# A new opening of a two-block transformer kernel: order of the first transfers, the first panel by high products first, bucket rows as a plain transfer, bias rows moved

## The chip, the core and the metric

The kernel runs on one core of one Trainium2 chip. The metric is the device time of one execution in microseconds (us), as the median of the runs made. TensorE does the matrix products, VectorE and ScalarE the elementwise work, GpSimd a few small steps, and SyncE issues most transfers. In rows of the profile they are PE, DVE, ACT, POOL and SP; PEld is TensorE's weight load.

## What is computed

Two blocks on 256 tokens of width 1024, all in float32. The first has two attention branches (a windowed one, and one with three dilated groups), each with biases by relative position from a table of 32 buckets; the second block has two layers with another table. The opening of the program is the first norm and the first projections:

```python
h = rms_norm(x, norm_gain[layer])
proj = h @ w_in[layer]
qa, ka, va, qb, kb, vb, ga, gb, mg = jnp.split(proj, split_idx, axis=-1)
...
qa = head_rms_norm(qa.reshape(bsz, S, A_Q_HEADS, HEAD_DIM), q_norm_a[layer]) * scale
ka = head_rms_norm(ka.reshape(bsz, S, A_KV_HEADS, HEAD_DIM), k_norm_a[layer])
va = va.reshape(bsz, S, A_KV_HEADS, HEAD_DIM)
ya, _ = banded_attention(qa, ka, va, A_WINDOW, 1, rel_bias[:, :A_Q_HEADS], sink_a[layer])
...
bias = bias_table[t5_bucket(rel * stride)]
```

## The kernel before

**Products in parts.** Each float32 operand is split into a high part (rounded to the matmul's own type, float32r) and a low part (the rest), and each product is made of three matmuls: high by high, high by low, low by high. Weights arrive in halves of 128 x 2048 elements (1 MB) in a ring of six slots. For each half ScalarE rounds the high part (`round_half`, L569) into one of three high slots, and VectorE subtracts to get the low part (`low_half`, L611). The first half of the first panel is done in two pieces (L566, L567, L604, L607).

**Panels.** A panel is 256 tokens by 512 output columns, in one of two PSUM buffers that take turns: `qa` in panel buffer 0, `kava` (256 columns) in buffer 1, `qb0` in buffer 0 again, `qb1` in buffer 1. `rows_out` writes a panel: for each of eight chunks k of the inner dimension and two groups b of tokens it issues the three matmuls (L921, L922, L923), 48 in all. Before its first matmul it waits until the buffer is evicted. After some chunks it runs other work (`after`), by the chunk's number.

**The head norm.** `qa`, `kava`, `qb0` to `kb2` are normed by head. Once the panel is done, ScalarE writes its squares (L1512, scaled by `rstd`, the row norm of x), VectorE sums them (L1884), GpSimd takes the inverse root (L2407 and L2409, `inverse_root`, with a drain between the two), and VectorE writes the normed heads to `tok` (L1894). Only then is the panel buffer free. Later TensorE transposes the heads (`turn_heads`) and ScalarE evicts them (`evict_heads`, L1451).

**The first work.** ScalarE's queue brings `ident` (the identity for transposes) and `first` (gains); SyncE's queue brings x in two pieces, three halves of weights, four small bias tables, and more halves. TensorE waits for `ident` and `first`, then transposes x in four groups of four (L971); ScalarE evicts each with the gain as the high part (L1393) and VectorE makes the low part (L1803). The row norm of x goes ScalarE (L1365), GpSimd (L2407, L2409, L2417).

**Bias rows.** `onehot`, 65 x 4608 elements, says for each relative position which bucket it has. GpSimd's queue brings it (L2412) once the second half of weights has landed, and the transfer rounds it to float32r. Nine matmuls of the table with it (L1029, `head_bias_row`) give nine tiles of bias rows, which ScalarE evicts (L1421, `evict_bias_row`) and, after the third panel, stores to memory (`store_bias_rows`). `BIAS_AT` says after which panel and chunk each is done: the first after the last chunk of `qa`, the other eight after the eight chunks of `kava`. These tiles, those of x and those of the turned heads share three PSUM tiles in the order of `FIRST_TILES`.

## Time and profile before

| | |
|---|---|
| three runs | 1227.75, 1228.25, 1226.32 us; median 1227.75 |
| the profiled execution | 1226.56 us, of which 1224.8 us are the span between its first and last instruction |
| mean granted clock of TensorE | 0.989 |

The span is the time from the first to the last instruction. The profile of one execution gives for each engine its instructions with their start and duration. "Idle before" with an arrow names what ended the idle time of the engine.

### The profile page before, as it was taken

What the parts mean: (1) busy time and instruction counts of PE and PEld (TensorE: products, weight loads), DVE (VectorE), ACT (ScalarE), POOL (GpSimd) and SP (SyncE); (2) the same over time, 40 slices, a digit from 0 to 9 for tenths busy, and PEclk for the clock granted to TensorE, in tenths of its full rate; (3) what the DMA queues carried; (4) which work ended last, traced back from release to release, by engine and by line L of the source; (5) the groups of instructions that cost most, each with busy time, mean ns of one, the idle gap of its engine ahead of it and who ended that gap; (6) DMA issues with size and microseconds to landing.
All of it is one profiled execution on the core that took longest, in us unless ns stands there. A gap on an engine that the chain in (4) does not pass through costs nothing.

```text
span 1224.8 us, 17214 instructions
## 1 busy us (share of the span) xinstructions
PE 1174.8 (96%) x6879; PEld 1013.7 (83%) x6879; DVE 825.6 (67%) x1317; ACT 571.1 (47%) x701; POOL 46.0 (4%) x56
## 2 busy tenths in 40 slices
PE   6999998999999998899999999999998899999996
PEld 5888887887998776687999888998776778999885
DVE  4665465556689768887677554698678787776542
ACT  5645564454425745453534433535745443444331
POOL 0232000000000000000000000000000000000000
PEclk9999999999999999899999999999999999999998
DMA  9656653436545667454555655556557554554640
GB/s 313 210 183 234 219 156 120 134 132 257 173 146 206 176 179 193 141 175 169 176 193 183 205 196 196 167 172 221 158 158 189 154 175 169 179 198 174 217 144 35
DMA packets 41344, 219.73 MB, mean 179 GB/s; under 512 B 4311, under 2 KB 14039, under 8 KB 16615
## 3 DMA queue, kind: packets, MB, share of 16 engines
q1 hardware_dynamic: 39104, 204.62, 48.8%
q0 software_dynamic: 1824, 13.78, 5.9%
q8 instruction: 55, 0.90, 0.3%
q10 hardware_dynamic: 336, 0.22, 0.1%
q14 instruction: 25, 0.20, 0.0%
...
## 4 chain that ended last, share of the span: by engine, by line
PE 77%; DVE 11%; issue 3%; ACT 3%; DVEq 2%; DMA 2%; POOL 0%; POOLq 0%; ACTq 0%
PE panel L921 16%; PE panel L923 15%; PE panel L922 15%; PE panel L944 7%; PE panel L943 7%; PE panel L942 7%; DVE area L2075 3%; PE tile L971 3%; DVE ring_parts L611 3%; ACT ring_parts L569 1%; DMA ring_parts<-in_w_layers_dram 1%; PE heads_out L1132 1%; DVEq L2076 1%; PE panel L961 1%; PE panel L960 1%
## 5 line engine op out<-in xcount | busy, mean ns | idle before, releaser
L611 DVE TENSOR_TENSOR ring_parts<-ring,ring_parts 128x2048 fp32r<-128x2048 f32 (+1 forms) x173 | 388.0, 2254 | 172.5 <-ACT ring_parts L569 162.1
L569 ACT ACTIVATE ring_parts<-ring 128x2048 fp32r<-128x2048 f32 (+1 forms) x185 | 348.1, 1888 | 241.3 <-PE panel L923 184.2
L921 PE MATMUL panel<-ring_parts,hT_high 128*128 128x512 f32 (+2 forms) x688 | 282.5, 411 | 11.7 <-DMA ring_parts<-in_w_layers_dram 8.5
L923 PE MATMUL panel<-ring_parts,hT_low 128*128 128x512 f32 (+2 forms) x688 | 267.4, 389 | 0.0
L922 PE MATMUL panel<-ring_parts,hT_high 128*128 128x512 f32 (+2 forms) x688 | 266.7, 388 | 0.0
L942 PE MATMUL panel<-hT_high,ring_parts 128*128 128x256 f32 x704 | 199.4, 283 | 0.0
L944 PE MATMUL panel<-hT_high,ring_parts 128*128 128x256 f32 x704 | 199.3, 283 | 0.0
L943 PE MATMUL panel<-hT_low,ring_parts 128*128 128x256 f32 x704 | 199.3, 283 | 0.0
L921 PEld LDWEIGHTS panel<-ring_parts,hT_high 128*128 128x128 f32 x688 | 131.3, 191 | 44.8 <-issue 11.8
L923 PEld LDWEIGHTS panel<-ring_parts,hT_low 128*128 128x128 f32 x688 | 130.9, 190 | 27.5
L921 PE MATMUL panel<-ring_parts,area_parts 128*128 128x512 f32 x384 | 150.6, 392 | 0.0
L922 PE MATMUL panel<-ring_parts,area_parts 128*128 128x512 f32 x384 | 149.9, 390 | 0.0
L922 PEld LDWEIGHTS panel<-ring_parts,hT_high 128*128 128x128 f32 x688 | 131.6, 191 | 20.3
L923 PE MATMUL panel<-ring_parts,area_parts 128*128 128x512 f32 x368 | 143.7, 391 | 0.0
L942 PEld LDWEIGHTS panel<-hT_high,ring_parts 128*128 128x128 f32 x704 | 135.2, 192 | 0.0
L943 PEld LDWEIGHTS panel<-hT_low,ring_parts 128*128 128x128 f32 x704 | 135.2, 192 | 0.0
L944 PEld LDWEIGHTS panel<-hT_high,ring_parts 128*128 128x128 f32 x704 | 135.2, 192 | 0.0
L2075 DVE SCALAR_TENSOR_TENSOR area<-area,cw 128x256 f32<-128x256 f32 x240 | 100.2, 479 | 2.9
L921 PEld LDWEIGHTS panel<-ring_parts,area_parts 128*128 128x128 f32 x384 | 72.2, 188 | 15.2
L922 PEld LDWEIGHTS panel<-ring_parts,area_parts 128*128 128x128 f32 x384 | 72.2, 188 | 15.0
L923 PEld LDWEIGHTS panel<-ring_parts,area_parts 128*128 128x128 f32 x368 | 69.1, 188 | 14.8
L1706 ACT ACTIVATE area_parts<-area 128x1024 fp32r<-128x1024 f32 x16 | 17.0, 1060 | 98.7 <-DVE area L2374 98.7
...
## 6 DMA issues: line engine op xcount, KB each, us to landing
ring<-in_w_layers_dram SPq DMA_DIRECT2D x140, 1024.0 KB, 4.9
ring<-in_w_first_dram SPq DMA_DIRECT2D x40, 1024.0 KB, 5.2
ring_parts<-in_w_layers_dram POOLq DMA_DIRECT2D x12, 1024.0 KB, 8.7
...
area<-in_gains_dram SPq DMA_DIRECT2D x3, 512.0 KB, 5.8
```

The lines of the kernel that those rows point to most:

```text
L569: act.activation(ring_lo[:, SLOTS + hi, 0:w], ring[:, slot, 0:w], ACT.Copy).then_inc(high_ready, 1)
L611: g.tensor_tensor(ring_lo[:, slot, 0:w], ring[:, slot, 0:w], ring_lo[:, SLOTS + hi, 0:w], ALU.subtract).then_inc(low_ready, 1)
L921: pe.matmul(ps[:, b, 0:width], high, hi[:, k, :], start=first, stop=False)
L922: pe.matmul(ps[:, b, 0:width], high, lo[:, k, :], start=False, stop=False)
L923: mm = pe.matmul(ps[:, b, 0:width], low, hi[:, k, :], start=False, stop=last)
L942: pe.matmul(to, hi[:, k, cols], hT_hi[:, k, :], start=(k == 0), stop=False)
L943: pe.matmul(to, hi[:, k, cols], hT_lo[:, k, :], start=False, stop=False)
L944: mm = pe.matmul(to, lo[:, k, cols], hT_hi[:, k, :], start=False, stop=(k == KC - 1))
L960: pe.matmul(to, hi[:, k, cols], hT_lo[:, k, :], start=False, stop=False, skip_group_check=True)
L971: mm = pe.transpose(ps[0:rows, i * P:(i + 1) * P], source(i), ident[:, :])
L1706: act.activation(hidden_parts()[0][:, 4 * i:4 * i + 4, :], sq[:, i % 2, :].rearrange("p (k t) -> p k t", k=4), ACT.Copy).then_inc(squares_ ...
L2075: v.scalar_tensor_tensor(acc[:, c, :], src, cw[:, c, j:j + 1], acc[:, c, :], ALU.mult, ALU.add)
```

## The change

1. **Transfers.** `first` goes to the head of SyncE's queue; TensorE waits for `ident` alone. The first half of weights comes as two transfers of 0.5 MB. `onehot` comes on SyncE's queue as a plain transfer, after the fourth half; ScalarE rounds it in place in two pieces of 65 x 2304 (`round_bucket_rows`). GpSimd issues no transfer in the first block. The small tables come after the sixth half.
2. **Constants and padding.** ScalarE runs one tiny activation as soon as the constants are there. TensorE runs two matmuls of 256 columns on zeros before the first transposes and two between the second and the third group (`keep_clock`).
3. **First panel.** The first half's high part is rounded by VectorE (`first_rounded`), not by ScalarE; ScalarE evicts all four groups of x in a row. `first_panel` issues for each half eight high-by-high matmuls, then eight with the low part of x, then eight with the low part of the weights, instead of three by turns.
4. **Bias rows.** They are done in `qb0` (after chunks 2, 3, 4, 6, 7) and `qb1` (after chunks 0 to 3). `turn_heads(0)` moves from chunk 3 to chunk 5 of `qb0`, the tables' parts (`bias_table_parts`) to the end of `kava` in VectorE's program, and the store to the end of `qb1`.
5. **After `qa`.** ScalarE rounds the half `qb0/0` ahead of the squares of `qa`, and the bucket rows behind them; VectorE makes the low part of `qb0/0` ahead of the sums of `qa`.

```diff
-BIAS_AT = {("qa", KC - 1): 0, **{("kava", k): k + 1 for k in range(KC)}}
-FIRST_TILES = (by_columns("x") + [f"bias{i}" for i in range(9)]
-               + [t for p in NORMED for t in transposed(p)] + plan_tiles(FIRST_PLAN, units_first())
+BIAS_AT = {**{("qb0", k): k - 2 for k in (2, 3, 4)}, ("qb0", 6): 3, ("qb0", 7): 4, **{("qb1", k): k + 5 for k in range(4)}}
+FIRST_TILES = (by_columns("x") + [f"bias{i}" for i in range(3)] + transposed("qa") + [f"bias{i}" for i in range(3, 5)]
+               + transposed("kava") + [f"bias{i}" for i in range(5, 9)] + [t for p in NORMED[2:] for t in transposed(p)] + plan_tiles(FIRST_PLAN, units_first())
                + transposed("yB") + by_columns("m") + by_columns("n"))
...
+            sp.dma_start(first[:, :], a["first"]).then_inc(first_loaded, 16)
             sp.dma_start(x[:, 0, :], sorted_x[0]).then_inc(x_loaded[0], 16)
             sp.dma_start(x[:, 1, :], sorted_x[1]).then_inc(x_loaded[1], 16)
...
-            for i in range(3):
+            slot = part_1.turn("half", "qa/0")[0]
+            sp.dma_start(ring[:, slot, 0:HALF // 2], a["w_first"][0][:, 0:HALF // 2]).then_inc(first_half_loaded, 16)
+            sp.dma_start(ring[:, slot, HALF // 2:HALF], a["w_first"][0][:, HALF // 2:HALF]).then_inc(half_loaded[slot], 16)
+            for i in range(1, 4):
+                load_first(i)
+            sp.dma_start(one("onehot")[0:2 * BUCKETS + 1, :], a["onehot"]).then_inc(onehot_loaded, 16)
+            for i in range(4, SLOTS):
                 load_first(i)
             for copy in range(2):
                 tabs = one("tabs")[BUCKETS * copy:BUCKETS * (copy + 1), :]
                 sp.dma_start(tabs[:, 0:32], a["rel_bias"]).then_inc(table_loaded, 16)
                 sp.dma_start(tabs[:, 32:40], a["rel_table"]).then_inc(table_loaded, 16)
-            for i in range(3, SLOTS):
-                load_first(i)
...
+            def keep_clock(n):
+
+                for _ in range(n):
+                    pe.matmul(tile[TILES - 1][:, 0:TOKENS], tok[:, 0, 0:P], tok[:, 0, 0:TOKENS], start=True, stop=True)
+
+            pe.wait_ge(pad_ready, PADS)
+            keep_clock(2)
+            pe.wait_ge(ident_loaded, 16)
...
+                for i in range(2):
+                    ks = range(4 * i, 4 * i + 4)
+                    low, high = (ring_lo[:, s, :].rearrange("p (k n) -> p k n", k=4)
+                                 for s in (part.turn("half", f"qa/{i}")[0], SLOTS + part.turn("high", f"qa/{i}")[0]))
+                    pe.wait_ge(x_high, 2 * i + NB)
                     if i == 0:
-                        pe.wait_ge(x_loaded[b], 16)
-                    turn(part, f"x{b}{i}", lambda c: x[:, b, (4 * i + c) * P:(4 * i + c + 1) * P])
+                        pe.wait_ge(first_high, 1)
+                    else:
+                        pe.wait_ge(high_ready, 2)
+                    for k in ks:
+                        if k == 2:
+                            pe.wait_ge(first_high, 2)
+                        product(k, hT_hi, high, first=k == 0)
+                    columns_ready(part, "x", i)
+                    for k in ks:
+                        product(k, hT_lo, high)
+                    if i == 0:
+                        pe.wait_ge(first_low, 1)
+                    else:
+                        pe.wait_ge(low_ready, 2)
+                    for k in ks:
+                        if k == 2:
+                            pe.wait_ge(low_ready, 1)
+                        mm = product(k, hT_hi, low, last=k == KC - 1)
+                    mm.then_inc(half_used if i == 0 else done, 1)
+
+            turn_x(0)
+            keep_clock(2)
+            turn_x(1)
...
                 if p == "qb0":
-                    between[3] = lambda: turn_heads(0)
-                rows_out(part, p, of_h, two_halves(p), 256 if p == "kava" else 512,
-                         ready=(lambda i: columns_ready(part, "x", i)) if p == "qa" else None, after=between)
+                    between[5] = lambda: turn_heads(0)
+                if p == "qa":
+                    first_panel()
+                else:
+                    rows_out(part, p, of_h, two_halves(p), 256 if p == "kava" else 512, after=between)
...
-            act.dma_start(ident[:, :], a["ident"]).then_inc(loaded, 16)
-            act.dma_start(first[:, :], a["first"]).then_inc(loaded, 16)
-            act.wait_ge(loaded, 16 * 2)
+            act.dma_start(ident[:, :], a["ident"]).then_inc(ident_loaded, 16)
+            act.wait_ge(pad_ready, PADS)
+            act.activation(brs[:, 0, 0:1], zero, ACT.Identity)
+            act.wait_ge(first_loaded, 16)
...
+            act.sem_inc(high_ready, 1)
+            for i in range(2):
+                for b in range(NB):
+                    evict_x(i, b)
+            for n in range(1, HI_SLOTS):
+                round_half(act, part, n)
             for b in range(NB):
                 act.wait_ge(x_loaded[b], 16)
                 row_squares(b, b)
-            for n in range(2, HI_SLOTS):
-                round_half(act, part, n)
+
+            def round_bucket_rows():
+
+                act.wait_ge(onehot_loaded, 16)
+                for i in range(2):
+                    of = slice(AREA_1["onehot"][0] + i * ROW // 2, AREA_1["onehot"][0] + (i + 1) * ROW // 2)
+                    act.activation(area_r[0:2 * BUCKETS + 1, of], area[0:2 * BUCKETS + 1, of], ACT.Copy).then_inc(onehot_rounded, 1)
...
                     if s == 4:
-                        if p == "qb0":
-                            evict_heads(0)
                         round_after(act, part, f"{p}/0")
+                    elif s == 6 and p == "qb0":
+                        evict_heads(0)
                     if (p, s) in BIAS_AT:
                         evict_bias_row(BIAS_AT[p, s])
                     for e in FIRST_PLAN.get((p, s), []):
@@ -1502,8 +1560,10 @@
                 ps = panel_of(act, part, p)
                 if n == 0:
                     act.wait_ge(rstd_ready, 1)
-                elif n == 2:
+                elif n == 3:
                     store_bias_rows()
+                if n == 0:
+                    round_after(act, part, "qa/1")
                 if n < len(NORMED):
                     for b in range(NB):
...
-                round_after(act, part, f"{p}/1")
+                if n == 0:
+                    round_bucket_rows()
+                else:
+                    round_after(act, part, f"{p}/1")
...
+            name, slot, _, hi = places(part, 0)
+
+            def first_rounded(i):
+                at = slice(i * HALF // 2, (i + 1) * HALF // 2)
+                v.wait_ge(half_loaded[slot] if i else first_half_loaded, 16)
+                v.tensor_copy(ring_lo[:, SLOTS + hi, at], ring[:, slot, at]).then_inc(first_high, 1)
+
+            first_low_tile(0, 0)
+            for i in range(2):
+                first_rounded(i)
+            first_low_tile(0, 1)
             low_half(v, part, 0)
             for b in range(NB):
                 first_low_tile(1, b)
-            low_half(v, part, 1)
-            bias_table_parts()
-            for n in range(2, HI_SLOTS):
+            for n in range(1, HI_SLOTS):
                 low_half(v, part, n)
             v.wait_ge(rstd_ready, 1)
...
@@ -1875,6 +1947,10 @@
                         lows_to(part, f"{p}/0")
                     for e in FIRST_PLAN.get((p, s), []):
                         step_first(*e)
+                if n == 0:
+                    lows_to(part, "qa/1")
+                elif n == 1:
+                    bias_table_parts()
                 if n < len(NORMED):
                     nh = 2 if p == "kava" else 8
                     for b in range(NB):
@@ -1883,8 +1959,6 @@
                             v.wait_ge(head_rstd, n)
                         v.tensor_reduce(hs[:, b, 0:nh], squares_of[:, b, 0:nh * HD].rearrange("p (h d) -> p h d", d=HD),
                                         AX.X, ALU.add).then_inc(head_sum, 1)
-                    if n == 0:
-                        lows_to(part, "qa/1")
                     ps = panel_of(v, part, p)
...
-            g.wait_ge(half_loaded[1], 16)
-            g.dma_start(parts(AREA_1["onehot"], 0, ROW)[0:2 * BUCKETS + 1, :], a["onehot"]).then_inc(onehot_loaded, 16)
             g.wait_ge(pad_ready, PADS)
```

ScalarE's program from the last half of `kava` to the squares of `kava`, before. Here `panel0_done` is the end of `qa`, `tile1_done` a bias row, and L569 rounds a half:

```order
L569 ACTIVATE ring_parts<-ring 128x1024 [waits half3_loaded,half_used,constant_fill_ready]
L1421 ACTIVATE area<-tile 8x2x256 [waits tile1_done]
L1512 ACTIVATE area<-panel,stat 128x512 [waits row_rstd_ready,panel0_done]
L1512 ACTIVATE area<-panel,stat 128x512
L569 ACTIVATE ring_parts<-ring 128x2048 [waits half4_loaded,panel0_done]
L1421 ACTIVATE area<-tile 8x2x256 [waits tile2_done]
L1421 ACTIVATE area<-tile 8x2x256 [waits tile0_done]
...
L569 ACTIVATE ring_parts<-ring 128x2048 [waits half5_loaded,half_used]
```

The same place in the changed kernel (L568 rounds a half, L1572 writes squares, L1464 rounds the bucket rows):

```order
L568 ACTIVATE ring_parts<-ring 128x1024 [waits half3_loaded,half_used,constant_fill_ready]
L568 ACTIVATE ring_parts<-ring 128x2048 [waits panel0_done,half4_loaded,row_rstd_ready]
L1572 ACTIVATE area<-panel,stat 128x512 x2
L1464 ACTIVATE area_parts<-area 65x2304 [waits bucket_rows_loaded]
L1464 ACTIVATE area_parts<-area 65x2304
L568 ACTIVATE ring_parts<-ring 128x2048 [waits half5_loaded,half_used]
L1572 ACTIVATE area<-panel,stat 128x128 [waits head_sums_ready,panel1_done]
L1572 ACTIVATE area<-panel,stat 128x128 [waits head_sums_ready]
```

The rounding of `qb0/0` (half4) now stands before the two squares of `qa` instead of behind them; the two pieces of bucket rows stand between these and the rounding of `qb0/1` (half5); the bias rows are gone from here.

VectorE's program from the low part of the second half of `kava` to the sums of `kava`, before (L1884 sums the squares, L1894 writes the normed heads and so frees the panel):

```order
L611 TENSOR_TENSOR ring_parts<-ring,ring_parts 128x1024 [waits high_part_ready,row_rstd_ready]
L1884 TENSOR_REDUCE stat<-area 128x8 [waits head_squares_ready] x2
L611 TENSOR_TENSOR ring_parts<-ring,ring_parts 128x2048 [waits high_part_ready]
L1894 SCALAR_TENSOR_TENSOR tok<-panel,stat 128x512 [waits head_rstd_ready,panel0_done]
L1894 SCALAR_TENSOR_TENSOR tok<-panel,stat 128x512
L611 TENSOR_TENSOR ring_parts<-ring,ring_parts 128x2048 [waits heads_normed,high_part_ready]
L1884 TENSOR_REDUCE stat<-area 128x2 [waits head_rstd_ready,head_squares_ready] x2
```

The same place in the changed kernel (L610 is the low part, L1960 the sum, L1968 the normed heads, L1808 to L1812 the tables' parts):

```order
L610 TENSOR_TENSOR ring_parts<-ring,ring_parts 128x1024 [waits high_part_ready,row_rstd_ready]
L610 TENSOR_TENSOR ring_parts<-ring,ring_parts 128x2048 [waits high_part_ready]
L1960 TENSOR_REDUCE stat<-area 128x8 [waits head_squares_ready] x2
L1968 SCALAR_TENSOR_TENSOR tok<-panel,stat 128x512 [waits head_rstd_ready,panel0_done]
L1968 SCALAR_TENSOR_TENSOR tok<-panel,stat 128x512
L610 TENSOR_TENSOR ring_parts<-ring,ring_parts 128x2048 [waits heads_normed,high_part_ready]
L1808 CAST area_parts<-area 32x40 [waits bias_tables_loaded]
L1809 CAST area_parts<-area 1x40
L1810 CAST area_parts<-area 32x40
L1812 TENSOR_TENSOR area_parts<-area,area_parts 32x40
L1960 TENSOR_REDUCE stat<-area 128x2 [waits head_rstd_ready,head_squares_ready] x2
```

The low part of `qb0/0`, 128 x 2048, has moved from behind the sums of `qa` to before them, and the tables' parts from the first panel to behind the low part of `qb0/1`.

TensorE's program around the first matmul of `qb0`, before (8x512 is a bias row, 128x256 is `kava`, 128x512 is `qb0`):

```order
L921 MATMUL panel<-ring_parts,hT_high 128x256
L922 MATMUL panel<-ring_parts,hT_high 128x256
L923 MATMUL panel<-ring_parts,hT_low 128x256
L921 MATMUL panel<-ring_parts,hT_high 128x256
L922 MATMUL panel<-ring_parts,hT_high 128x256
L923 MATMUL panel<-ring_parts,hT_low 128x256
L1029 MATMUL tile<-area_parts 8x512 [waits tile0_evicted]
L921 MATMUL panel<-ring_parts,hT_high 128x512 [waits low_part_ready,panel0_evicted]
L922 MATMUL panel<-ring_parts,hT_high 128x512
```

The same place in the changed kernel:

```order
L923 MATMUL panel<-ring_parts,hT_high 128x256
L924 MATMUL panel<-ring_parts,hT_high 128x256
L925 MATMUL panel<-ring_parts,hT_low 128x256
L923 MATMUL panel<-ring_parts,hT_high 128x512 [waits low_part_ready,panel0_evicted]
L924 MATMUL panel<-ring_parts,hT_high 128x512
L925 MATMUL panel<-ring_parts,hT_low 128x512
...
L924 MATMUL panel<-ring_parts,hT_high 128x512
L925 MATMUL panel<-ring_parts,hT_low 128x512
L1079 MATMUL tile<-area_parts 8x512 [waits tile1_evicted,bias_table_parts_ready,bucket_rows_rounded]
L923 MATMUL panel<-ring_parts,hT_high 128x512
```

No bias row stands in `kava` any more, so the first matmul of `qb0`, which waits for buffer 0 to be evicted, follows directly on `kava`'s 48; the first bias row comes 18 matmuls later.

## Rows read from the trace of the kernel before

**Rows 1.** The page, busy time of TensorE and its share of the span.

```profile
PE 1174.8 (96%) x6879; PEld 1013.7 (83%) x6879; DVE 825.6 (67%) x1317; ACT 571.1 (47%) x701; POOL 46.0 (4%) x56
```

**Rows 2.** Timeline of TensorE in the opening: start us, us, what, idle before.

```profile
5.30 3.08 PE L971 MATMUL tile<-ident,x 128*128 128x128 f32 x12 [5.30 <-DMA first<-in_first_dram]
10.15 1.11 PE L971 MATMUL tile<-ident,x 128*128 128x128 f32 x4 [1.77 <-DVE hT_low L1803]
12.41 0.77 PE L921 MATMUL panel<-ring_parts,hT_high 128*128 128x512 f32 x1 [1.14 <-DVE ring_parts L604]
...
24.73 0.39 PE L923 MATMUL panel<-ring_parts,hT_low 128*128 128x512 f32 x1
25.99 0.41 PE L1029 MATMUL tile<-area_parts 65*8 65x512 f32 x1 [0.87 <-DMA area_parts<-in_onehot_dram]
26.23 0.28 PE L921 MATMUL panel<-ring_parts,hT_high 128*128 128x256 f32 x1
26.35 0.29 PE L922 MATMUL panel<-ring_parts,hT_high 128*128 128x256 f32 x1
...
30.83 0.39 PE L1029 MATMUL tile<-area_parts 65*8 65x512 f32 x1 [0.87 <-ACT area L1421]
...
34.62 0.40 PE L1029 MATMUL tile<-area_parts 65*8 65x512 f32 x1
34.85 0.40 PE L921 MATMUL panel<-ring_parts,hT_high 128*128 128x512 f32 x1
```

**Rows 3.** Timeline of ScalarE, same columns.

```profile
6.50 1.28 ACT L1393 ACT_TABLE_LOAD   x1 [6.50 <-PE tile L971]
...
27.25 1.26 ACT L1512 ACTIVATE area<-panel,stat 128x512 f32<-128x512 f32 x2 [0.23 <-POOL stat L2417]
28.40 1.91 ACT L569 ACTIVATE ring_parts<-ring 128x2048 fp32r<-128x2048 f32 x1
```

**Rows 4.** Timeline of VectorE, same columns.

```profile
28.33 1.27 DVE L1884 TENSOR_REDUCE stat<-area 128x8 f32<-128x512 f32 x2
30.35 2.29 DVE L611 TENSOR_TENSOR ring_parts<-ring,ring_parts 128x2048 fp32r<-128x2048 f32 x1 [0.74 <-ACT ring_parts L569]
33.19 1.41 DVE L1894 SCALAR_TENSOR_TENSOR tok<-panel,stat 128x512 f32<-128x512 f32 x2 [0.55 <-POOL stat L2409]
```

**Rows 5.** Timeline of GpSimd in the opening, and in both later stages.

```profile
18.07 0.18 POOL L2407 TENSOR_SCALAR stat<-stat 128x2 f32<-128x2 f32 x1 [4.98 <-issue]
26.13 0.72 POOL L2409 TENSOR_TENSOR stat<-stat 128x2 f32<-128x2 f32 x1 [7.87 <-issue]
26.94 0.22 POOL L2417 TENSOR_SCALAR stat<-stat 128x2 f32<-128x2 f32 x1
...
452.70 1.67 POOL L2409 TENSOR_TENSOR stat<-stat 128x8 f32<-128x8 f32 x1 [0.63 <-issue]
...
590.81 0.69 POOL L2409 TENSOR_TENSOR stat<-stat 128x2 f32<-128x2 f32 x1 [0.16 <-issue]
```

**Rows 6.** Transfers issued from 0 to 60, and from 6 to 12 us: us to landing.

```profile
area_parts<-in_onehot_dram POOLq DMA_DIRECT2D x1, 1170.0 KB, 13.7
x<-in_x_dram SPq DMA_DIRECT2D x2, 512.0 KB, 4.6
...
ring<-in_w_first_dram SPq DMA_DIRECT2D x2, 1024.0 KB, 19.1
```

**Rows 7.** Stretches: us, PE busy (x instructions), PEld, DVE, ACT, POOL, PEclk, DMA, GB/s.

```profile
12.40:15.70 3.30, 3.29 (x8) 2.62 (x9) 3.07 (x9) 3.30 (x8) 0.69 (x1) 1.00 1.01 349
15.70:25.10 9.40, 9.40 (x42) 7.43 (x40) 4.14 (x6) 4.11 (x7) 0.18 (x1) 1.00 1.09 265
...
200.00:203.40 3.40, 3.40 (x13) 1.83 (x12) 0.48 (x1) 0.10 (x1) 0.00 (x0) 0.51 0.00 0
498.50:503.80 5.30, 5.26 (x17) 4.62 (x18) 5.08 (x14) 0.49 (x1) 0.00 (x0) 0.50 0.92 170
```

**Rows 8.** Timeline of TensorE at one of its later waits.

```profile
198.70 0.66 PE L971 MATMUL tile<-ident,area 128*128 128x128 f32 x4 [3.53 <-ACT area L1488]
```

40 lines of the change are left out of this document (19 added, 21 removed).

## The prediction

> **What bounds the kernel now.** The page comes first: TensorE is busy for 1174.8 of 1224.8 us [rows 1], so a microsecond that TensorE idles or gains in the opening stays in the total, unless a later wait absorbs it. The timeline of TensorE then shows what the opening loses [rows 2]. It starts at 5.30, released by `first`. It stands still for 1.77 us before the last group of x, for 1.14 us before `qa` (its first product needs a low part of the weights), for 0.87 us before the first bias row (bucket rows not landed) and for 0.87 us at the fifth (its tile not evicted). `qa` is issued from 12.41 to about 24.96 and its last record ends at 25.12. `qb0` starts at 34.85, right behind the last bias row.
>
> A second chain runs beside it, and the reader is to see it in ScalarE, VectorE and GpSimd [rows 3 to 5]. Buffer 0 holds `qa` until its heads are normed, and `qb0` needs that buffer. The squares start at 27.25, the sums run from 28.33 to 29.60, the normed heads are written from 33.19 to 34.60. That is 0.25 us before `qb0` starts. So before the change TensorE and this chain arrive together, and this is what decides the change: making TensorE early at `qb0` gains nothing unless the chain gets early too.
>
> **The opening up to the end of `qa`.** `first` no longer gates TensorE, but x is now issued one transfer later and needs 4.6 us to land [rows 6]; I keep a start near 5.6 (5.3 to 6.0). Sixteen transposes cost 0.26 us each, as twelve took 3.08 [rows 2]: 4.2 us. Two padding matmuls of 256 columns stand between them; no row shows one here, their bounds are nothing and two transposes each (twice the columns), 0.5, and I take the upper one since the path is full: 1.0. With 0.2 for the second piece of x the groups end at 11.0. The table load of 1.28 us [rows 3] leaves the path from the first transpose to the first high part, and the low parts are wanted 16 matmuls later, so `qa` starts at 11.0 instead of 12.41. Rounding 128 x 1024 on VectorE has no row; the subtraction of 128 x 2048 takes 2.29 [rows 4], half of that is 1.15, and even this hides, as nothing asks for the low part of the weights before the seventeenth matmul.
>
> The pace is 9.40 / 42 = 0.224 us once the clock is up; the first 8 took 3.3 us, 1.5 more than at that pace [rows 7]. The column of the granted clock says 1.00 there, but the spacing of 0.41 is that of the lower level (1.2 GHz). TensorE now works without a pause from some 6 us on, and I let the clock rise early in `qa`: 0.7 lost (0 to 1.5). `qa` takes 11.0 + 0.7 and is done at 22.8 instead of 25.12: 2.3 us earlier.
>
> **`kava`.** Its 48 matmuls follow at 0.12 (26.23 to 26.35 [rows 2]), 5.8 us, with no bias row and neither wait of 0.87 between. TensorE stands before `qb0` at 28.5, where it was at 34.85.
>
> **The chain that frees buffer 0.** It starts at 22.8, and its order is new. ScalarE first rounds `qb0/0`, 1.91, to 24.8; in that time no square is written. VectorE makes that half's low part, 2.29, to 27.1, and only then the sums, 1.27, to 28.4. From the end of the sums to the normed heads is 33.19 - 29.60 = 3.59, through GpSimd, to 32.0; the normed heads take 1.41, to 33.4. TensorE starts `qb0` at 33.5. The chain costs 10.6 us from the end of `qa`; with squares and sums first it would be 7.4 (27.25 to 34.60 [rows 3, 4]). **First term: 33.5 - 34.85 = -1.35 us**, with 5.0 us of standing still at `qb0`.
>
> This needs the row norm of x before 22.8. Before, it came at 27.16, since GpSimd stood still for 7.87 us between its two steps, until 26.13; the transfer of the bucket rows, issued at 12.3, took 13.7 us to land, at 26.0 [rows 5, 6]. The drain between the steps waits for the transfer, I read. The later rows agree: 0.63 us where a GpSimd transfer was just landing, 0.16 where none was out [rows 5]. With it gone, GpSimd's first step stands where it stood, near 18, since x's squares are as early as before, and the norm is ready by 19.5 (18.07 + 0.18 + 0.16 + 0.72 + 0.22). The Trainium skill has another rule that would fit the same row: "GPSIMD Engine Reference", section 2.1, says that the first call of newly loaded GpSimd code costs about 6 us that no instruction of the profile shows. By the row's reading the norm is hidden; by the page's it would come at about 25, an estimate from its figure, and everything would be 2 us later. The 7.87 us are closer to the landing than to that figure, so I keep the first.
>
> **The bias rows.** Nine matmuls of 0.23 us (34.62 to 34.85 [rows 2]) leave `kava`, where the chain would have hidden them, and stand in `qb0` and `qb1`, where TensorE is the bound. **Second term: +2.1 us.** The tables' parts and the rounded bucket rows are no wait: the tables follow the low part of `qb0/1`, and their four operations on 40 columns get 0.2 each, what two columns take on GpSimd [rows 5]: 33.4 + 2.3 + 0.8 = 36.5; the first bias row is asked for 18 matmuls after 33.5, at 37.6. The bucket rows' rounding, 65 x 2304 twice, is priced between nothing and 1.91 x 2304 / 2048 = 2.15 each; at the upper end ScalarE is done at 30.2, ahead of need.
>
> **The clock.** TensorE has not stood still for more than 1.8 us in the opening so far. Now it does for 5.0 us. The waits of this length later in the trace are followed by the lower level: after 3.53 us idle [rows 8] the granted clock is 0.51 for 3.4 us, and in another place 0.50 for 5.3 us, with TensorE busy [rows 7]. At half speed that loses 1.7 or 2.65 us. **Third term: +1.7 us** (0 to 2.65; the one that starts in the idle time costs less).
>
> **A new tile wait.** In `qb1` the second bias row uses the tile of `kava`'s first turned heads. After the end of `qb0` ScalarE evicts a bias row (512 wide as one square is, half of 1.26: 0.6), writes squares (1.26), rounds a half (1.91) and only then evicts these heads (a quarter as wide: 0.3): 4.1 us. TensorE asks after two transposes, twelve matmuls and a bias row: 3.4 us. **Fourth term: +0.7 us** (0 to 0.8).
>
> **Sum.** -1.35 + 2.1 + 1.7 + 0.7 = +3.15 us on the profiled 1226.56. That execution is 1.2 below the median of the three runs (1227.75), and sum on median is 1230.9, sum on profile 1229.7; I say 1230.5. A change of 0.2% (2.45 us) is about what a measurement tells from none.
>
> **Rivals.**
> - *The clock stays up at `qb0`, and the tile is free in time* (17 in 100): -1.35 + 2.1 = +0.75, so 1228.5, not slower. For it speaks that the 1.77 us wait [rows 2] left the pace alone; against it rows 7 and 8. It decides from an idle time under about 3 us, and 5.0 is far.
> - *`kava` covers the chain, so that `qb0` does not wait* (5): the first term is -6.35 and the third falls away, -6.35 + 2.1 + 0.7 = -3.55, 1224, faster. It decides from a chain under 5.8 us after `qa`, `kava`'s length. Its own rows make 10.6, and GpSimd's part and the normed heads alone 3.59 + 1.41.
> - *The norm of x comes late anyway* (10): GpSimd stands still for its 8 us at its first use. 17.5 + 9.1 (18.07 to 27.16 [rows 5]) is 26.6 for the norm, 3.8 later than `qa`'s end, and the rounding waits behind it: +6.9, 1234.5.
> - *`qb0/0` lands late* (13). Ahead of its end stand about 6.3 MB (x, five halves or part halves and the 1.2 MB of bucket rows). At 349 GB/s that is 18 us, landing near 21, in time; at 265, seen while the bucket rows were under way [rows 7], 24 us, landing near 26, and 3.4 us late: +6.5, 1234. In the trace the halves issued next to them took 19.1 [rows 6]. I take the faster rate, since the slow one came with the rounding transfer. The Trainium skill ("DMA: Bandwidth & Descriptors", section "Why a DMA increments its semaphore by 16 and not by 1") says that a transfer of 65 rows on such a queue is split over 13 of the 16 engines, as 13 is the largest divisor of 65 up to 16. No run here shows it yet; the estimate from it would make that transfer a fifth longer, under 1 us.
>
> The forecast itself holds 50 in 100, with its own range 1228.8 to 1232.5 (each bound of terms one and three). 5 are left for cases that I do not see, 3 of them gains. The range 1227.0 to 1234.0 takes in the first two rivals and part of the late transfers. Slower by over 0.2%: six tenths of the forecast, all of the last two rivals: 0.52. Faster: 0.08. Within: 0.40.
>
> **What would show it.** `qa` done near 22.8; then ScalarE in the order half, squares, bucket rows; an idle time of TensorE of about 5 us before `qb0`'s first matmul, released by VectorE's normed heads near 33.4; a granted clock of 0.5 soon after; GpSimd with a short gap at its first root, near 18; a wait of 0.7 us in `qb1` released by ScalarE. I am wrong if `qb0` starts before 31 or without a wait, if GpSimd's gap stays near 8 us, or if the pace after the wait is the full one.

## The result, and the profile after

The changed kernel takes 1235.42 us (median of 4 runs, 1233.38 to 1236.57), the kernel before beside it 1227.42 (1226.32 to 1228.25): a ratio of 1.0064, 95% interval 1.0046 to 1.0081. It is slower by 8.0 us, more than forecast (1230.5) and outside the range (to 1234.0).

The profiled execution took 1236.57 us with a span of 1234.8. The profile's page gives TensorE 5.3 us more of busy time than [rows 1]:

```profile
PE 1180.1 (96%) x6887; PEld 1017.6 (82%) x6887; DVE 827.2 (67%) x1320; ACT 574.3 (47%) x702; POOL 46.8 (4%) x55
```

The timeline of TensorE, columns as in [rows 2]:

```profile
5.59 2.28 PE L973 MATMUL tile<-ident,x 128*128 128x128 f32 x8 [2.10 <-DMA x<-in_x_dram]
...
10.94 2.46 PE L1039 MATMUL panel<-ring_parts,hT_high 128*128 128x512 f32 x8
...
20.50 1.98 PE L1039 MATMUL panel<-ring_parts,hT_high 128*128 128x512 f32 x8
38.64 0.80 PE L923 MATMUL panel<-ring_parts,hT_high 128*128 128x512 f32 x1 [10.41 <-DVEq L1979]
39.23 0.63 PE L924 MATMUL panel<-ring_parts,hT_high 128*128 128x512 f32 x1
...
57.69 0.40 PE L1079 MATMUL tile<-area_parts 65*8 65x512 f32 x1 [0.64 <-ACT area L1509]
...
207.52 1.12 PE L973 MATMUL tile<-ident,area 128*128 128x128 f32 x4 [3.53 <-ACT area L1546]
```

`qa` starts at 10.94 and its last record ends at 22.48. `kava` follows until 28.2, and then TensorE stands still for 10.41 us. `qb0` starts at 38.64, not at 33.5. The last row is the end of a wait that both kernels have ([rows 8]: same 3.53 us, same releaser); it is used below as a mark behind the opening. It stands 8.82 us later than before (207.52 - 198.70). ScalarE, VectorE and GpSimd say what TensorE waited for:

```profile
19.05 1.06 ACT L568 ACTIVATE ring_parts<-ring 128x1024 fp32r<-128x1024 f32 x1 [0.48 <-DMA ring<-in_w_first_dram]
28.12 1.91 ACT L568 ACTIVATE ring_parts<-ring 128x2048 fp32r<-128x2048 f32 x1 [8.01 <-DMA ring<-in_w_first_dram]
29.94 1.25 ACT L1572 ACTIVATE area<-panel,stat 128x512 f32<-128x512 f32 x2
31.08 4.12 ACT L1464 ACTIVATE area_parts<-area 65x2304 fp32r<-65x2304 f32 x2
```

```profile
30.06 2.29 DVE L610 TENSOR_TENSOR ring_parts<-ring,ring_parts 128x2048 fp32r<-128x2048 f32 x1 [7.22 <-ACT ring_parts L568]
32.27 1.27 DVE L1960 TENSOR_REDUCE stat<-area 128x8 f32<-128x512 f32 x2
37.11 1.41 DVE L1968 SCALAR_TENSOR_TENSOR tok<-panel,stat 128x512 f32<-128x512 f32 x2 [3.57 <-POOL stat L2483]
```

```profile
18.83 1.60 POOL L2481 TENSOR_SCALAR stat<-stat 128x2 f32<-128x2 f32 x1 [18.40 <-ACT tok L1417]
20.58 0.69 POOL L2483 TENSOR_TENSOR stat<-stat 128x2 f32<-128x2 f32 x1
21.36 0.22 POOL L2489 TENSOR_SCALAR stat<-stat 128x2 f32<-128x2 f32 x1
33.73 0.21 POOL L2481 TENSOR_SCALAR stat<-stat 128x16 f32<-128x16 f32 x1 [12.15 <-DVE stat L1960]
34.09 2.92 POOL L2483 TENSOR_TENSOR stat<-stat 128x16 f32<-128x16 f32 x1
```

Read the chain backwards. The normed heads (37.11) waited for GpSimd's root (34.09), this for the sums (32.27), these for the low part of `qb0/0` (30.06), this for ScalarE's rounding of it. And the rounding, at 28.12, waited 8.01 us for a transfer. Half 4 (`qb0/0`) was issued at 5.64 and took 22.4 us to land. That is the view of the transfers issued from 5.6 to 5.7:

```profile
ring<-in_w_first_dram SPq DMA_DIRECT2D x1, 1024.0 KB, 22.4
```

From the rounding to `qb0` the chain takes 10.5 us, as forecast (10.6). It only starts 5.3 us late. GpSimd had the norm of x ready at 21.6, without the gap of [rows 5]. The stretches show the rate at which the transfers came, and the granted clock:

```profile
14.00:22.50 8.50, 8.50 (x40) 7.06 (x39) 7.27 (x12) 5.61 (x7) 2.51 (x3) 1.00 1.02 218
...
32.20:38.64 6.44, 0.00 (x1) 0.01 (x1) 2.75 (x5) 6.44 (x6) 3.13 (x2) 0.50 0.86 361
38.64:42.50 3.86, 3.86 (x9) 3.09 (x10) 3.39 (x7) 0.67 (x1) 0.05 (x1) 0.51 0.09 38
42.50:50.00 7.50, 7.50 (x36) 5.76 (x35) 4.19 (x6) 3.45 (x4) 1.16 (x2) 1.00 0.34 111
```

From 14 to 22.5 us the 16 engines are all busy and move only 218 GB/s. From 32.2 the clock is granted at 0.5, for the rest of the wait and for the first 3.9 us of `qb0`, in which 9 matmuls are done.

### The profile page after: what moved, and what is told of

It is laid out like the page before. It is cut to its first block, busy times and chain, and to the rows that moved or that the text cites. A ratio compares the mean times of both kernels' runs of the same rounds, so it can differ in the third digit from the quotient of the medians.

```text
span 1234.8 us, 17239 instructions
## 1 busy us (share of the span) xinstructions
PE 1180.1 (96%) x6887; PEld 1017.6 (82%) x6887; DVE 827.2 (67%) x1320; ACT 574.3 (47%) x702; POOL 46.8 (4%) x55
## 4 chain that ended last, share of the span: by engine, by line
PE 77%; DVE 11%; DMA 3%; ACT 3%; DVEq 3%; issue 2%; POOL 1%; SPq 0%; POOLq 0%; ACTq 0%
PE panel L923 16%; PE panel L925 15%; PE panel L924 15%; PE panel L946 7%; PE panel L945 7%; PE panel L944 7%; DVE area L2149 3%; PE tile L973 3%; DVE ring_parts L610 3%; DMA ring<-in_w_first_dram 2%; ACT ring_parts L568 2%; DMA ring_parts<-in_w_layers_dram 1%; PE heads_out L1184 1%; DVEq L2150 1%; POOL stat L2483 1%
## 5 line engine op out<-in xcount | busy, mean ns | idle before, releaser
L610 DVE TENSOR_TENSOR ring_parts<-ring,ring_parts 128x2048 fp32r<-128x2048 f32 (+1 forms) x173 | 388.1, 2254 | 173.5 <-ACT ring_parts L568 169.0
L568 ACT ACTIVATE ring_parts<-ring 128x2048 fp32r<-128x2048 f32 (+1 forms) x185 | 347.9, 1886 | 248.2 <-PE panel L925 182.8
L923 PE MATMUL panel<-ring_parts,hT_high 128*128 128x512 f32 (+2 forms) x672 | 276.6, 412 | 21.3 <-DVEq L1979 10.4
L925 PE MATMUL panel<-ring_parts,hT_low 128*128 128x512 f32 (+2 forms) x672 | 261.8, 390 | 0.0
L924 PE MATMUL panel<-ring_parts,hT_high 128*128 128x512 f32 (+2 forms) x672 | 260.8, 388 | 0.0
L923 PEld LDWEIGHTS panel<-ring_parts,hT_high 128*128 128x128 f32 x672 | 128.7, 192 | 54.2 <-DVEq L1979 10.6
L925 PEld LDWEIGHTS panel<-ring_parts,hT_low 128*128 128x128 f32 x672 | 128.0, 191 | 26.9
L924 PEld LDWEIGHTS panel<-ring_parts,hT_high 128*128 128x128 f32 x672 | 128.9, 192 | 19.5
```

What stands on the lines that cost most here:

```text
L568: act.activation(ring_lo[:, SLOTS + hi, 0:w], ring[:, slot, 0:w], ACT.Copy).then_inc(high_ready, 1)
L610: g.tensor_tensor(ring_lo[:, slot, 0:w], ring[:, slot, 0:w], ring_lo[:, SLOTS + hi, 0:w], ALU.subtract).then_inc(low_ready, 1)
L923: pe.matmul(ps[:, b, 0:width], high, hi[:, k, :], start=first, stop=False)
L924: pe.matmul(ps[:, b, 0:width], high, lo[:, k, :], start=False, stop=False)
L925: mm = pe.matmul(ps[:, b, 0:width], low, hi[:, k, :], start=False, stop=last)
```

## The experiments

All ratios are to the kernel before, run beside it on the same chip. The edits are shortened: where one changes the number of transfers, the waits for them change too, and that is left out. Half 4 is `qb0/0`, half 5 `qb0/1`. Times of landing are read from the ScalarE row that waits for the half.

**1. The halves first.** The two halves are issued ahead of the bucket rows:

```
 for i in range(1, 4): load_first(i)
+for i in range(4, SLOTS): load_first(i)
 sp.dma_start(one("onehot")[0:2 * BUCKETS + 1, :], a["onehot"]).then_inc(onehot_loaded, 16)
-for i in range(4, SLOTS): load_first(i)
```

> Order of issue alone: half 4 (qb0/0) and half 5 (qb0/1) are issued ahead of the bucket rows, nothing else is changed. Theory L (the changed kernel is slow because half 4 lands at 28.1 us, behind and beside the bucket rows): half 4 lands before 22.5, ScalarE rounds it right after qa, the chain of 10.5 us starts at 22.5, qb0 starts near 33.3 instead of 38.64, and about 5 us of 8 are given back: 1230 to 1231. Rival C (the chain through GpSimd or the clock gate is what costs, and the half's landing only hides behind it): qb0 stays past 37, time near 1235. Bucket rows land later by some 3 us and may hold the first bias row, asked for 18 matmuls after qb0 begins; I expect no wait there.

Measured: 1230.14 us, ratio 1.0023 (1.0014 to 1.0033). In the timelines of ScalarE and TensorE:

```profile
22.19 1.92 ACT L568 ACTIVATE ring_parts<-ring 128x2048 fp32r<-128x2048 f32 x1 [2.98 <-PE panel L1039]
...
32.71 0.79 PE L923 MATMUL panel<-ring_parts,hT_high 128*128 128x512 f32 x1 [4.95 <-DVEq L1979]
...
202.17 1.11 PE L973 MATMUL tile<-ident,area 128*128 128x128 f32 x4 [3.53 <-ACT area L1546]
```

The half is there when `qa` ends (its rounding waits for TensorE, not for a transfer), and `qb0` starts 10.5 us later with an idle time of 4.95. This is the forecast's own picture (33.5, 5.0 us, 1230.5), and this order of two lines is the difference between forecast and result. The late half is shown as the cause of 5 of the 8 us (3.0 are left).

**2. The bucket rows as 64 rows and 1 row.**

```
-sp.dma_start(one("onehot")[0:2 * BUCKETS + 1, :], a["onehot"]).then_inc(onehot_loaded, 16)
+sp.dma_start(one("onehot")[0:64, :], a["onehot"][0:64, :]).then_inc(onehot_loaded, 16)
+sp.dma_start(one("onehot")[64:65, :], a["onehot"][64:65, :]).then_inc(onehot_loaded, 16)
```

> The bucket rows come as two transfers, 64 rows and 1 row, instead of one of 65. Theory S (one transfer of 65 rows is split over fewer of the DMA engines than one of 64): the packets of 18432 bytes spread evenly over all engines, the rows land about a fifth sooner, half 4 by 1 to 1.5 us sooner, total near 1234. Theory P (the pace is set by the partitions written to: rows of 18 KB to 64 partitions move at half the rate, however many engines carry them): packets still take 1.2 us or more and the small ones beside them 0.6, half 4 lands within 0.5 us of 28.1, and the total stays at 1235.

Measured: 1233.36 us, ratio 1.0051 (1.0038 to 1.0064), half 4 rounded from 24.99. By the first profile of the changed kernel that would be 3.1 us sooner, but a second one of the same kernel (run 13) also has 24.99. For the total this is inconclusive. The trace's record of each packet does show the split: of the 65 packets of 18432 bytes, at most 13 were under way at one moment in the changed kernel and 16 here, if overlaps of under 20 ns aren't counted (15 and 18 with them). And the rate isn't higher for it:

```profile
14.00:22.50 8.50, 8.50 (x44) 7.23 (x43) 6.53 (x11) 4.30 (x7) 2.66 (x3) 1.00 0.97 212
```

212 GB/s, where the changed kernel has 218, and 243 in its second profile. The split over fewer engines isn't what makes the rate low.

**3. Squares first.** After `qa` ScalarE writes the squares before it rounds `qb0/0`, and VectorE sums them before it makes that half's low part (one call moved on each engine).

```
 # ScalarE, n == 0                       # VectorE, n == 0
-round_after(act, part, "qa/1")          -lows_to(part, "qa/1")
 row squares of both row tiles            sums of both row tiles
+round_after(act, part, "qa/1")          +lows_to(part, "qa/1")
```

> The order on ScalarE and VectorE after qa alone: squares and sums of qa first, the rounding of qb0/0 and its low part behind them. Theory L (the squares wait behind a rounding whose half lands late): the chain starts at 22.5 and takes 7.4 us, so buffer 0 is free near 30; but qb0 needs the rounded half, landing at 28.1 plus 1.9, 30.0, and its low part, 2.3 more, only later in the row of products if the product order allows it, else 32.4. qb0 starts at 30.3 to 32.6, time 1228 to 1230. Rival C (the norm's chain through GpSimd is the bound): qb0 stays past 37.

Measured: 1228.42 us, ratio 1.0012 (1.0003 to 1.0021).

```profile
28.75 1.91 ACT L568 ACTIVATE ring_parts<-ring 128x2048 fp32r<-128x2048 f32 x1 [5.14 <-DMA ring<-in_w_first_dram]
...
34.42 0.79 PE L923 MATMUL panel<-ring_parts,hT_high 128*128 128x512 f32 x1 [6.37 <-DVEq L1978]
...
202.83 0.66 PE L973 MATMUL tile<-ident,area 128*128 128x128 f32 x4 [3.53 <-ACT area L1546]
```

The half lands as late as in the changed kernel (28.75), and still `qb0` starts 4.2 us sooner, since the squares, the sums and GpSimd's root were done meanwhile (GpSimd at 27.8): from the half's rounding to `qb0` it takes 5.7 us in place of 10.5. I had expected 30.3 to 32.6: I left out that the normed heads queue behind the low part on VectorE. The total is what I expected.

**4. The bucket rows by GpSimd's rounding transfer,** as in the kernel before (waiting for the landing of half 1), and ScalarE's two roundings of them left out:

```
+g.wait_ge(half_loaded[1], 16)
+g.dma_start(parts(AREA_1["onehot"], 0, ROW)[0:65, :], a["onehot"]).then_inc(onehot_loaded, 16)
```

> The bucket rows by GpSimd's rounding transfer as in the kernel before (behind the landing of half 1), ScalarE's two roundings of them left out; the rest as in the changed kernel. Theory D (GpSimd's drain waits for its own transfer): the gap between its first two steps is 6 to 8 us again, the norm of x comes with the landing of the rows, past 22.5. If the rounding transfer slows the others as the plain one does, half 4 still lands between 24 and 28. Expected total 1233 to 1237. If the gap stays at 0.15 us with the transfer out, theory D falls.

Measured: 1236.23 us, ratio 1.0074 (1.0061 to 1.0087). GpSimd:

```profile
17.62 1.74 POOL L2478 TENSOR_SCALAR stat<-stat 128x2 f32<-128x2 f32 x1 [4.14 <-issue]
26.56 0.72 POOL L2480 TENSOR_TENSOR stat<-stat 128x2 f32<-128x2 f32 x1 [7.20 <-issue]
```

The gap is back, 7.20 us, and ends 1.1 us behind the last packet of the rows (25.5; before the change 24.9 and 26.13, 1.2 us). The drain waits for GpSimd's own transfer. So this part of the change did what the prediction said, and without it the norm of x comes 6 us later (27.6 against 21.6). The total moves little from the changed kernel's, since here the late norm holds the same rounding (27.67) about as long as the late half does there (28.12).

**5. Both orders:** the edits of runs 1 and 3, the tables issued ahead of the bucket rows too, and the bucket rows rounded behind `qb0/1`, with ScalarE in the steps of `kava`:

```
-if n == 0: round_bucket_rows()
 if s == 4:
     round_after(act, part, f"{p}/0")
+    if n == 1: round_bucket_rows()
```

> Both orders together: all six halves and the tables are issued ahead of the bucket rows, squares and sums of qa come first and the rounding and the low part of qb0/0 behind them; the bucket rows are rounded after the half of kava. Theory L: half 4 lands before 22.5, so squares 22.4 to 23.6, sums to 24.4, GpSimd to 27.9, the low part of qb0/0 is done at 27.9 too, normed heads to 29.3: qb0 starts at 29.4 instead of 32.71 (half first) or 34.42 (squares first), its idle time is about 1.5 us and the clock stays up: -3.3 and -1.7 against the run with the halves first, 1225.2, just under the kernel before. Rival K (the clock falls here whatever the wait at qb0): 1226.8. Rival T (the first bias row then waits for the bucket rows, which land at 29.3 or later and are rounded until 35 or more): the first bias row, asked for at about 33.5, waits 2 us: 1227.

Measured: 1225.42 us, ratio 0.9973 (0.9962 to 0.9984), faster than the kernel before.

```profile
29.11 0.50 PE L923 MATMUL panel<-ring_parts,hT_high 128*128 128x512 f32 x1 [1.39 <-DVEq L1979]
...
36.22 0.40 PE L1079 MATMUL tile<-area_parts 65*8 65x512 f32 x1 [2.73 <-ACT area_parts L1464]
...
199.06 1.11 PE L973 MATMUL tile<-ident,area 128*128 128x128 f32 x4 [3.53 <-ACT area L1546]
```

`qb0` starts at 29.11 with 1.39 us of standing still, and no stretch at 0.5 follows until 198 us. Rival T came true in this profile: the first bias row waited 2.73 us for the rounding.

**6. The same bytes to 128 partitions.** The transfer of the bucket rows is replaced by one of weights to all 128 partitions, of the same size. The right bucket rows, and with them the position bias, are left out.

```
+sp.dma_start(one("onehot")[:, 0:2048], a["w_first"][38]).then_inc(onehot_loaded, 16)
+sp.dma_start(one("onehot")[:, 2048:2304], a["w_first"][39][:, 0:256]).then_inc(onehot_loaded, 16)
```

> The transfer of the bucket rows is replaced by one of the same size to all 128 partitions (2304 columns each, in packets of 8192 and 1024 bytes, taken from later weights); the right bucket rows and so the position bias are left out. All else stands. Theory P (rows of 65 partitions halve the pace of everything under way): the total rate stays near 400 GB/s, half 4 lands by about 22.5 instead of 28.1, qb0 starts near 33.5 and the total is near 1230. Rival Q (it is the bytes themselves ahead of half 4): half 4 lands at 26 or later.

Measured: 1230.34 us in one run. The stretch, ScalarE and TensorE:

```profile
14.00:22.50 8.50, 8.50 (x41) 7.07 (x41) 7.27 (x12) 5.50 (x8) 2.65 (x3) 1.00 1.02 406
...
22.34 1.92 ACT L568 ACTIVATE ring_parts<-ring 128x2048 fp32r<-128x2048 f32 x1 [3.00 <-PE panel L1040]
...
32.86 0.53 PE L924 MATMUL panel<-ring_parts,hT_high 128*128 128x512 f32 x1 [4.94 <-DVEq L1980]
```

406 GB/s where the changed kernel has 218, and the half is in time though the same bytes stand ahead of it. The number of bytes is not the cause.

**7. The 65 rows in column pieces** (packets of at most 8192 bytes):

```
+for at in (0, 2048, 4096):
+    to = min(at + 2048, ROW)
+    sp.dma_start(one("onehot")[0:65, at:to], a["onehot"][:, at:to]).then_inc(onehot_loaded, 16)
```

> The same 65 bucket rows in three transfers of 2048, 2048 and 512 columns, so in packets of at most 8192 bytes instead of 18432. Theory G (the size of the packets makes the others slow: large ones hold the engines): half 4 lands 3 us or more sooner, total near 1231. Theory P (it is the 65 partitions): the packets of these rows take about 0.6 us each where the weights' take 0.31, half 4 lands within 1 us of 28.1, total near 1235.

Measured: 1234.13 us, ratio 1.0053 (1.0035 to 1.007); 267 GB/s from 14 to 22.5, half 4 rounded from 24.20. That is below all five landings of the unsplit form with this issue order (24.99 to 28.75, run 13), by less than these differ. The rate is above the 218 and 243 of the changed kernel and far from 406: the size of the packets isn't what brings it down.

**8. Weights to 65 partitions,** in the pieces of run 7: the source of run 6, the places of the bucket rows. The position bias is again left out.

```
+for i, at in enumerate((0, 2048, 4096)):
+    w = min(2048, ROW - at)
+    sp.dma_start(one("onehot")[0:65, at:at + w], a["w_first"][37 + i][0:65, 0:w]).then_inc(onehot_loaded, 16)
```

> In the changed kernel, rows 0 to 64 of later weights (2048, 2048 and 512 columns) are brought to the places of the bucket rows, in the order and in the packet sizes of the run with the rows in columns; the right bucket rows, and with them the position bias, are left out. Theory P (the 65 partitions written to set the pace): the rate falls to 200 to 250 GB/s for 6 us as there, half 4 lands near 24.2. Rival R (it is where the bucket rows lie in memory that makes them slow to read): the rate stays near 400 and half 4 lands by 22.5, as with the same bytes to 128 rows.

Measured: 1235.4 us in one run.

```profile
14.00:22.50 8.50, 8.50 (x40) 7.04 (x39) 7.27 (x13) 5.68 (x7) 2.66 (x3) 1.00 1.02 261
...
26.36 1.92 ACT L568 ACTIVATE ring_parts<-ring 128x2048 fp32r<-128x2048 f32 x1 [6.68 <-DMA ring<-in_w_first_dram]
```

261 GB/s. From the same tensor, in packets of up to the same size, 128 partitions take 406 and 65 take 261. So it is the partitions written to, and neither the source nor the packets nor (run 2) the split over engines. No run writes to another set of 64 or 65 partitions, so whether their number counts or which they are isn't shown.

**9. 18 padding matmuls in the wait** before `qb0`:

```
+if p == "kava":
+    for _ in range(18):
+        pe.matmul(tile[TILES - 1][:, 0:TOKENS], ident[:, :], x[:, 0, 0:TOKENS], start=True, stop=True)
```

> 18 padding matmuls of 256 columns (0.48 us each at the full clock, 8.6 us) are added behind kava, in the wait of 10.4 us before qb0; nothing else is changed. Theory K (the wait brings the clock down to 0.5 afterwards and that costs 1.9 us): no granted clock of 0.5 between 30 and 45, qb0 starts at the same 38.6, total 1233.5. Rival: the clock falls all the same, total 1235.4.

Measured: 1233.85 us, ratio 1.0045 (1.0031 to 1.0059). They ended at 35.1, a wait of 2.43 us was left, and the clock was still granted at 0.5 for 3.4 us from 37.2. `qb0` started at 37.50 and the mark stands at 206.04, 168.54 us between. A miss: the lower clock stayed, so its price can't be read from this run.

**10. 24 padding matmuls.** The edit of run 9, with this line:

```
-    for _ in range(18):
+    for _ in range(24):
```

> 24 padding matmuls instead of 18 behind kava. With 18 a wait of 2.43 us was left at qb0 and the granted clock still went to 0.5, for 3.4 us in place of 10.2. With 24 they end near 37.6, when the chain is through, so that TensorE stands still for under 0.5 us. Theory K (it is the standing still that brings the clock down, and the second half of what a late half costs): no granted clock of 0.5 between 30 and 50; half 4 landed 1 us sooner in the run with 18, so by its landing at 27 the total is 1233.85 - 1.7 = 1232.1, by a landing at 28 it is 1233.2. Rival: the clock falls at this place whatever TensorE does, 1234 to 1235.

Measured: 1236.93 us, ratio 1.0079 (1.006 to 1.0099).

```profile
27.24 10.53 PE L1099 MATMUL tile<-x,ident 128*128 128x256 f32 x48
37.41 0.58 PE L923 MATMUL panel<-ring_parts,hT_high 128*128 128x512 f32 x1
37.83 0.39 PE L924 MATMUL panel<-ring_parts,hT_high 128*128 128x512 f32 x1
...
204.65 1.11 PE L973 MATMUL tile<-ident,area 128*128 128x128 f32 x4 [3.53 <-ACT area L1549]
...
37.41:42.00 4.59, 4.59 (x22) 3.67 (x21) 2.74 (x10) 0.00 (x0) 1.21 (x2) 1.00 0.03 11
426.40:433.20 6.80, 5.90 (x17) 4.94 (x18) 6.09 (x24) 5.64 (x11) 0.00 (x0) 0.50 0.24 100
```

`qb0` follows the padding without a wait, at the full clock, and from its start to the mark it takes 167.24 us where the changed kernel takes 168.88 (207.52 - 38.64). So the lower clock cost 1.6 us, and the padding kept it up. It gave nothing back in all: half 4 landed at 25.48 here and the chain was through at 35.9, the padding held `qb0` for 1.5 us more. And a stretch at the lower clock appears at 426.4, with TensorE busy for 5.90 of 6.80 us. It begins in a wait for weights of 2.49 us (to 427.30) that is 1.23 us long in the changed kernel; there no such stretch follows, but run 3 has one of 3.4 us near this place, at 423.0, behind a wait of 1.26. From the mark to the end of the next long wait, near 486, it takes 281.3 us here where the changed kernel takes 278.8. Why the weights come later there stays open. With it the median is 3.7 us above my higher figure: the price of the clock is shown at `qb0`, and not in the total.

**11 and 12. The better order, refined.** Run 11 (`c3`) takes run 5 and brings the bucket rows as 64 rows in two pieces of 2304 columns and row 65 alone ahead of them; the first bias row waits for the first piece, the fifth for the second. Run 12 (`c4`) also evicts `kava`'s turned heads before the rounding of a half, where they stood behind it.

```
 # both                                           # run 12, ScalarE
+act.wait_ge(onehot_second if i else ..., ...)    +if n == 2: evict_heads(n - 1)
+if i in (0, 4):                                   round_after(act, part, f"{p}/1")
+    pe.wait_ge(onehot_rounded, 2 if i else 1)    +if 2 < n <= len(NORMED): evict_heads(n - 1)
```

> The kernel with both orders, and the bucket rows as 64 rows in two pieces of 2304 columns (and row 65 alone ahead of them), each rounded when it lands; the first bias row waits for the first piece only, the fifth for the second. In the kernel with both orders the first bias row waited 2.73 us for the roundings, which began with the landing at 32.0. The first piece now lands near 26, rounded by 29, the second near 29.5, rounded by 32; no wait at a bias row: 1225.4 - 2.7 = 1222.7. Rival: the second piece is late (past 34) and the fifth bias row waits: 1224 to 1225.

> As the run before it, and after the end of qb0 ScalarE evicts kava's turned heads ahead of the rounding of a half instead of behind it. The wait of 0.64 us of TensorE in qb1 (for the tile of these heads) goes: 1222.1. Rival: the half rounded 0.3 us later is waited for instead: 1222.7.

Measured: 1224.74 us, ratio 0.9978 (0.9969 to 0.9987), and 1223.94 us, ratio 0.9976 (0.9966 to 0.9986). TensorE in run 11 and in run 12:

```profile
29.48 0.50 PE L927 MATMUL panel<-ring_parts,hT_high 128*128 128x512 f32 x1 [1.39 <-DVEq L1984]
...
46.78 0.40 PE L1084 MATMUL tile<-area_parts 65*8 65x512 f32 x1 [0.64 <-ACT area L1514]
...
196.60 1.11 PE L977 MATMUL tile<-ident,area 128*128 128x128 f32 x4 [3.53 <-ACT area L1551]
```

```profile
29.10 0.50 PE L927 MATMUL panel<-ring_parts,hT_high 128*128 128x512 f32 x1 [1.39 <-DVEq L1986]
...
195.45 0.66 PE L977 MATMUL tile<-ident,area 128*128 128x128 f32 x4 [3.53 <-ACT area L1551]
```

No bias row waits in either, and the wait of 0.64 us is gone in run 12: from `qb0` to the mark 167.12 and 166.35 us. The medians moved less than expected (1222.7 and 1222.1). Against run 5 the intervals overlap, so they are not shown to be better than it.

**13 and 14. A second profile** of the changed kernel and of run 5; the diff to each is empty.

> The changed kernel once more, for a second profile. Half 4 landed at 28.06 in the first and at 26.98 in the run with 18 padding matmuls, which is the same program up to there. Theory V: it lands between 26 and 29 and qb0 starts 10.5 us later; the late half is there in each execution, and its size varies by about 1 us. If it lands before 24.5, the late half is an accident of one execution and not the cause of the median.

> The kernel with both orders once more, for a second profile. Its median is 2.3 us below that of the kernel before, but in its profile TensorE comes to the wait of 3.53 us near 199 us 0.36 us later than in the profile of before. Theory V (the landing of the bucket rows differs from one execution to the next by a microsecond or more, and the first bias row waits for it): the landing, 32.0 us, and the start after that wait, 199.06, move together, earlier by 1 us or more. Rival: both stand within 0.3 us of the first profile, and the time is won behind the opening.

Measured, the changed kernel (1234.25 us) and then run 5 (1225.4):

```profile
24.99 1.91 ACT L568 ACTIVATE ring_parts<-ring 128x2048 fp32r<-128x2048 f32 x1 [6.50 <-DMA ring<-in_w_first_dram]
...
35.51 0.80 PE L923 MATMUL panel<-ring_parts,hT_high 128*128 128x512 f32 x1 [8.46 <-DVEq L1979]
...
204.65 1.11 PE L973 MATMUL tile<-ident,area 128*128 128x128 f32 x4 [3.53 <-ACT area L1546]
```

```profile
28.18 4.15 ACT L1464 ACTIVATE area_parts<-area 65x2304 fp32r<-65x2304 f32 x2 [0.96 <-DMA area<-in_onehot_dram]
...
29.44 0.50 PE L923 MATMUL panel<-ring_parts,hT_high 128*128 128x512 f32 x1 [1.38 <-DVEq L1979]
...
196.60 1.11 PE L973 MATMUL tile<-ident,area 128*128 128x128 f32 x4 [3.53 <-ACT area L1546]
```

Both landings move. Half 4's rounding waited for it until 28.12, 24.99, and in the three kernels with the same transfers up to there (runs 3, 9 and 10) until 28.75, 26.98 and 25.48: 2.5 to 6.3 us behind the end of `qa`, near 22.5, each time. In run 5 the bucket rows landed at 32.0 and now at 28.2, the first bias row waits for nothing, and the mark stands 2.46 us earlier. So run 5's first profile had a wait that not every execution has, which fits that runs 11 and 12 gain less over it than that profile let expect.

## Why the prediction was wrong

From `qb0`'s start to the mark, what is left is the terms behind the chain, and they come apart by subtraction:

| kernel | `qb0` starts | mark | between | what it has of the terms |
|---|---|---|---|---|
| before | 34.85 | 198.70 | 163.85 | none |
| run 12 | 29.10 | 195.45 | 166.35 | bias rows |
| run 11 | 29.48 | 196.60 | 167.12 | bias rows, tile wait |
| changed | 38.64 | 207.52 | 168.88 | bias rows, tile wait, clock |
| changed, again | 35.51 | 204.65 | 169.14 | the same |

**First term, -1.35 forecast, +3.8 measured (38.64 - 34.85; +0.7 in the second profile): this failed.** Its parts were right but one. `qa` started at 10.94 and ended at 22.48 (11.0 and 22.8), `kava` ended at 28.2 (28.5), the norm of x was ready at 21.6 (19.5 forecast, needed at 22.5), the chain from the rounding took 10.5 us (10.6). The start of `qa` owes something to luck: its 16 transposes took 3.7 us and not 4.2, and the padding between them 1.7 and not 1.0. The step that failed is "I take the faster rate, since the slow one came with the rounding transfer". The half landed 22.4 us after its issue, not near 21 us of the span but at 28.1 (25.0 in the second profile). The slow rate of [rows 7] belonged to the bucket rows, whoever brings them: 265 GB/s in the kernel before [rows 7], 218 and 243 in the two profiles of the changed one, 212 in run 2, 267 and 261 in runs 7 and 8, and 406 with the same bytes to 128 partitions (run 6); and `qb0/0` is in time when it goes first (run 1). The Trainium skill ("SBUF — State Buffer", section "Door 1: The DMA port swizzle") says that partitions 0 to 63 reach only half of the 16 ports through which transfers write. By that rule, an estimate, a transfer to 65 partitions runs at about half the rate. The traces agree as far as they go: 218 GB/s in all against 406, and the weights beside it slow down as well; they don't show the ports. The split over 13 engines, which the prediction cites from the Trainium skill ("DMA: Bandwidth & Descriptors", section "Why a DMA increments its semaphore by 16 and not by 1"), fits the count of packets under way, 13 against 16 (run 2). Without it the rate was no higher, 212 GB/s.

What happened is the prediction's fourth rival, with its mechanism and its mark (a half landing near 26, 3.4 us late, 1234); it was given 13 in 100, and a time 1.4 us too low.

**Second term, +2.1 forecast, +2.5 measured** (166.35 - 163.85). In the timeline of run 12 the nine bias rows take 2.16 us, 0.24 each; the other 0.3 lies between the panels' own matmuls, and its cause stays open. Right.

**Third term, +1.7 forecast, 1.8 to 2.0 measured** (168.88 and 169.14 less 167.12), and 1.6 by run 10. Right in size, though the wait was 10 us and not 5. The low clock began in the wait, at 32.2, and what counts is the part of it behind the start of `qb0`. That part differs: by the same subtraction run 1, with a wait of 4.95 us as forecast, pays 2.3 (169.46, the clock at 0.5 until 37.8), run 9 pays 1.4 and run 3 pays 1.3 (168.41). So the agreement at 1.7 is within a spread of 1.3 to 2.3, and in part luck.

**Fourth term, +0.7 forecast, 0.8 measured** (167.12 - 166.35; the row says 0.64). Right.

Sum at the mark: 3.8 + 2.5 + 1.8 + 0.8 = 8.9, against 8.82 read. It has to come out, as the last three were made by subtraction; the time per bias row, the row of 0.64 and run 10 are what bears them out. Behind the mark the profiled execution loses 1.2 us more (1234.8 - 207.52 against 1224.8 - 198.70). There the clock stays low for 6.8 us from 206.3, where the kernel before has 3.4 us from 200.0 [rows 7], behind the same wait. The medians differ by 8.0.

**The first rival fell:** the clock went low at `qb0`, and the tile was waited for. **The second rival fell** as forecast: where the chain starts at the end of `qa` (run 1), `kava` covers 5.6 of its 10.5 us. **The third rival fell:** GpSimd's first step took 1.60 us and the next began 0.15 later. (Its sum sets that step at 17.5, where the prediction's own row has 18.07; it came at 18.83.) The 7.87 us before the change were the wait of the drain for the transfer (run 4). The rule of about 6 us for the first call of new code ("GPSIMD Engine Reference", section 2.1, of the Trainium skill) isn't seen here: no gap of that length is left.

The new opening as such isn't the loss. `qa` ends 2.6 us earlier than before, and with the issue order and the squares' order of run 5 the same change is 0.27% faster than the kernel before (ratio 0.9962 to 0.9984).
